# Softmax division moved into the matrix that transposes P, in two attention stages of a fused fp32 block

## The reference, cut to what matters

```
# block 1: 6 query heads, 2 key/value heads, window of +-128, blocks of 128 queries see up to 3 blocks of keys
scores = einsum(q * 64**-0.5, k) + bias
m = maximum(max(scores), sink)                  # sink: one learned logit per head
p = exp(scores - m)
p = p / (sum(p) + exp(sink - m))
out = einsum(p, v)
# block 2, mixer A: 8 heads with a sink, causal window of 128 (up to 2 blocks of keys)
# block 2, mixer B: 8 heads without a sink, causal over all 1024 keys with a table of logits (up to 8 blocks)
```

## Time and profile before

| | us |
|---|---|
| median of 3 runs (lowest, highest) | 3511.18 (3509.3, 3518.65) |
| the profiled execution: its own time | 3517.96 |
| its span | 3516.2 |
| `att_bi`, from the first scores to the last value product | about 417 to 528 in the span |
| `att_ab`, band heads | about 2258 to 2362 |
| `att_ab`, wide heads | about 2362 to 2554 |

### The profile page before, as it was taken

How to read it: one execution, slowest core, us unless ns; L and a number is a source line. 1 busy time by engine, 2 the same in 40 slices (tenths; PEclk the granted TensorE clock), 3 DMA queues, 4 the chain that set the end, 5 groups by cost and what they waited for, 6 DMA issues and landing times.

```text
span 3516.2 us, 40420 instructions
## 1 busy us (share of the span) xinstructions
PE 3244.8 (92%) x15143; PEld 2633.6 (75%) x15143; DVE 1805.5 (51%) x2429; ACT 1213.0 (34%) x2329; POOL 1656.6 (47%) x1159
## 2 busy tenths in 40 slices
PE   6978889899999999999999999888898999999987
PEld 3865568677777787788887888866677788887875
DVE  6879662878885225655522131365526655532133
ACT  3135362444442113333412130265513334312132
POOL 3321116655557667644476642210056644476652
PEclk8989899999999999999999999998899999999998
DMA  5524414322324432223245234444242223245232
GB/s 189 117 99 137 122 49 174 126 90 72 123 75 147 185 122 78 85 78 126 72 161 209 96 124 138 150 109 120 60 165 67 86 78 126 72 161 211 104 125 86
DMA packets 286911, 414.58 MB, mean 118 GB/s; under 512 B 26536, under 2 KB 211051, under 8 KB 285589
## 3 DMA queue, kind: packets, MB, share of 16 engines
q1 hardware_dynamic: 218968, 240.41, 22.8%
q10 hardware_dynamic: 62812, 154.67, 11.6%
q0 software_dynamic: 4960, 17.22, 1.5%
HBM read 324.79 MB, written 93.75 MB: 119 GB/s over the span
## 4 chain that ended last, share of the span: by engine, by line
PE 71%; DVE 15%; ACT 7%; issue 4%; DMA 2%; ACTq 1%; POOL 1%; SPq 0%; DVEq 0%; POOLq 0%
PE PS L900 63%; PE PS L2361 4%; DVE pl_ab L2478 1%; DVE cset L1340 1%; DVE ss L1216 1%; DVE cset L1338 1%; DMA w_raw<-ffn_w_down 1%; DVE pt L769 1%; PE PS L836 1%; ACT ph_ab L2412 1%; PE PS L2344 1%; DVE h_lo L894 1%; ACT pr_ab L2399 1%; ACT act L743 1%; DVE cset L1452 1%
## 5 line engine op out<-in xcount | busy, mean ns | idle before, releaser
L1244 POOL TENSOR_TENSOR sl<-ss,sh 128x512 fp32r<-128x512 f32 x300 | 436.4, 1460 | 478.6 <-ACT sh L1231 477.4
L290 POOL TENSOR_TENSOR w_lo<-w_raw,w_hi 128x512 fp32r<-128x512 f32 x460 | 641.0, 1425 | 16.0
L286 POOL CAST w_hi<-w_raw 128x2048 fp32r<-128x2048 f32 x115 | 226.9, 1973 | 658.1 <-DMA w_raw<-w_in 200.3
L1452 DVE TENSOR_TENSOR cset<-cset,PS 128x512 f32<-128x512 f32 x360 | 236.3, 684 | 403.2 <-PE PS L900 355.7
L900 PE MATMUL PS<-h_hi,sh 128*128 128x512 f32 x960 | 378.8, 395 | 27.2 <-ACT cset L1390 25.3
L900 PE MATMUL PS<-h_lo,sh 128*128 128x512 f32 x960 | 376.3, 392 | 0.0
L900 PE MATMUL PS<-h_hi,sl 128*128 128x512 f32 x960 | 376.2, 392 | 0.0
L971 DVE TENSOR_TENSOR a_lo<-aT,a_hi 128x1024 fp32r<-128x1024 f32 x66 | 104.2, 1582 | 487.6 <-ACT a_hi L968 487.6
L900 PE MATMUL PS<-w_hi,a_hi 128*128 128x512 f32 x1056 | 329.3, 393 | 19.6 <-POOL w_lo L290 14.8
L1231 ACT ACTIVATE sh<-ss 128x512 fp32r<-128x512 f32 x285 | 180.1, 632 | 478.5 <-DVE ss L1216 478.2
L900 PE MATMUL PS<-w_lo,a_hi 128*128 128x512 f32 x1056 | 328.1, 392 | 0.0
(11 more groups left out here) (362 smaller groups left out, 6348.6 us busy)
## 6 DMA issues: line engine op xcount, KB each, us to landing
w_raw<-ffn_w_down SPq DMA_DIRECT2D x88, 512.0 KB, 4.2
sr<-ffn_w_gu SPq DMA_DIRECT2D x80, 512.0 KB, 5.1
ad<-cset ACTq DMA_DIRECT2D x66, 512.0 KB, 3.1
w_raw<-w_down SPq DMA_DIRECT2D x44, 512.0 KB, 4.3
xs<-px ACTq DMA_DIRECT2D x40, 512.0 KB, 2.6
sr<-w_up SPq DMA_DIRECT2D x40, 512.0 KB, 5.1
aT<-ad ACTq DMA_DIRECT2D x3, 5632.0 KB, 17.2
w_raw<-w_out SPq DMA_DIRECT2D x32, 512.0 KB, 4.4
```

Of the source, the lines that this page charges most:

```text
L286: e.tensor_copy(w_hi[b][:, 0:n], w_raw[b][:, 0:n]).then_inc(S("w_hi"), 1)
L290: op = e.tensor_tensor(w_lo[b][:, s], w_raw[b][:, s], w_hi[b][:, s].bitcast(F32), ALU.subtract)
L1244: e.tensor_tensor(s.lo[p][:], src, s.hi[p][:].bitcast(F32), ALU.subtract).then_inc(S("s_op"), 1)
L1452: e.tensor_tensor(out, out, PS[:, b, :], op).then_inc(S("s_ev"), 1)
```

## The change

The reciprocal is taken for each unit: DVE `share(m)`, between `score(m + 1)` and `low_(m - 1)`. POOL `diagonal(m)` writes `dg[m % 2]`, the identity times the unit's 128 reciprocals. PE multiplies `pr` by this matrix instead of transposing it with `ident`: an ordinary fp32 matmul. The result is P transposed and divided. So `sinks`, `denom`, `spread`, `spread_out`, `scale`, `rr` and `t` go. The sink is a column more of `pr` that POOL `sink_column(m)` writes ahead of the exponential. The values come out of PSUM ready: ACT `y_high` and DVE `y_low` write 64 rows each for every group. For that v is loaded with both halves of its 128 columns alike. The transposed P has three banks (4, 5, 7). `out_pe` waits at its start for the last but four of these splits, and for the last one only where it needs it.

```diff
             def turn_p(m):
                 d, b, k0, k1, chunks = s.units[m]
-                e.wait_ge(S("at_exp"), n + m + 1)
+                e.wait_ge(S("at_dg"), n + m + 1)
                 for q, c0, c1 in chunks:
-                    wait(e, S("at_lo"), s.ch0 + q - 1)
+                    if q >= 3:
+                        e.wait_ge(S("at_lo"), s.ch0 + q - 2)
+                    elif q == 2 and s is att_bi:
+                        e.wait_ge(S("gl_s"), 3)
                     for k in range(c0, c1):
-                        mm = e.transpose(PS[:, 4 + q % 2, (k - c0) * P:(k - c0 + 1) * P],
-                                         a.pr[m % 3][:, (k - k0) * P:(k - k0 + 1) * P], ident[:])
+                        mm = e.matmul(PS[:, TURN_BANK[q % 3], (k - c0) * P:(k - c0 + 1) * P],
+                                      a.pr[m % 3][:, (k - k0) * P:(k - k0 + 1) * P], a.dg[m % 2][:], start=True, stop=True)
                     mm.then_inc(S("at_tr"), 1)
...
             def y_high(g):
                 d = s.units[4 * g][0]
-                e.wait_ge(S("at_nrm"), g_ + g + 1)
-                e.activation(HI(d.slot, g % 2), a.t[g // 4 % 2][:, g % 2, :], ACT.Copy)\
-                 .then_inc(S("at_yh"), 1)
+                e.wait_ge(S("at_pv"), g_ + g + 1)
+                r = slice(d.half * HD, (d.half + 1) * HD)
+                e.activation(HI(d.slot, g % 2)[r], PS[r, 6, :], ACT.Copy).then_inc(S("at_yh"), 1)
...
-                if m % 4 == 0 and g:
-                    spread_out(g - 1)
-                if m % 4 == 2 and g and (g - 1) % 4 >= 2:
+                if m % 4 == 1 and g:
                     y_high(g - 1)
...
+            def share(m):
+                e.wait_ge(S("at_exp"), n + m + 1)
+                e.reciprocal(ast[:, RD, m % 8:m % 8 + 1], ast[:, DEN, m % 8:m % 8 + 1]).then_inc(S("at_rd"), 1)
...
                 if m + 2 < s.n:
                     score(m + 2)
-                if m % 4 == 1 and m > 1:
-                    scale(m // 4 - 1)
+                if m + 1 < s.n:
+                    share(m + 1)
+                if m % 4 == 2 and m > 2:
+                    y_low(m // 4 - 1)
                 low_(m)
...
+            def diagonal(m):
+                e.wait_ge(S("at_rd"), n + m + 1)
+                if m >= 2:
+                    e.wait_ge(S("at_tr"), s.unit_end(m - 2))
+                e.tensor_scalar(a.dg[m % 2][:], ident[:], ast[:, RD, m % 8:m % 8 + 1], None, ALU.mult).then_inc(S("at_dg"), 1)
+
+            sink_column(0)
+            sink_column(1)
+            e.wait_ge(S("w_used"), (G_OUT2 if s.z else G_OUT1)[0])
+            for m in range(s.n):
+                diagonal(m)
+                if m + 2 < s.n:
+                    sink_column(m + 2)
+                if s is att_bi and 1 <= m < 7:
+                    gated_low_pool(e, m - 1)
```

More of the change, by code:

```diff
@@ L1062, in out_act @@
         def out_act(e, p):
-            e.wait_ge(S("at_yl"), 6 if p == 0 else 22)
+            e.wait_ge(S("at_yl"), 12 if p == 0 else 44)
             if p == 0:
@@ L2363, in values @@
                 mm.then_inc(S("at_pv"), 1)
-            def spread(g):
-                e.wait_ge(S("at_rd"), g_ + g + 1)
-                wait(e, S("at_rc"), g_ + g)
-                for k in range(4):
-                    r = 4 * (g % 2) + k
-                    mm = e.transpose(PS[:, 7, k * P:(k + 1) * P], ast[:, RD, r:r + 1].to_broadcast([P, P]), ident[:])
-                mm.then_inc(S("at_r"), 1)
             if s is att_ab:
@@ L2383, in att_pe @@
                     turn_p(m)
-                else:
-                    spread(m // 4 - 1)
                 if m % 4 == 3:
@@ L2392, in att_pe @@
                     tab_pe(e, m - 12)
-            spread(s.n // 4 - 1)
         def exps(e, s, a, m):
-            _, _, k0, k1, _ = s.units[m]
-            x, r, n = a.pr[m % 3][:, 0:(k1 - k0) * P], m % 8, s.h0 * TT
+            d, _, k0, k1, _ = s.units[m]
+            w, r, n = (k1 - k0) * P, m % 8, s.h0 * TT
             e.wait_ge(S("at_s"), n + m + 1)
+            if d.sink is not None:
+                e.wait_ge(S("at_sk"), n + m + 1)
+                w += 1
+            x = a.pr[m % 3][:, 0:w]
             e.activation(x, x, ACT.Exp, scale=-1.0, bias=ast[:, NM, r:r + 1], accum_out=ast[:, DEN, r:r + 1])\
@@ L2477, in low_, with y_low @@
                     o = (slice(None), slice(c0 - kb0, c1 - kb0), slice(b % 4 * P, (b % 4 + 1) * P))
[L2478 removed]
+                    e.tensor_tensor(a.pl[o], PS[:, TURN_BANK[q % 3], 0:(c1 - c0) * P].rearrange("p (k n) -> p k n", n=P),
                                     a.ph[o].bitcast(F32), ALU.subtract).then_inc(S("at_lo"), 1)
[L2481 to L2498 removed]
+            def share(m):
+                e.wait_ge(S("at_exp"), n + m + 1)
+                e.reciprocal(ast[:, RD, m % 8:m % 8 + 1], ast[:, DEN, m % 8:m % 8 + 1]).then_inc(S("at_rd"), 1)
+            def y_low(g):
+                d = s.units[4 * g][0]
+                e.wait_ge(S("at_yh"), g_ + g + 1)
+                r = slice(d.half * HD, (d.half + 1) * HD)
+                e.tensor_tensor(LO(d.slot, g % 2)[r], PS[r, 6, :], HI(d.slot, g % 2)[r].bitcast(F32), ALU.subtract)\
+                 .then_inc(S("at_yl"), 1)
             score(0)
             score(1)
+            share(0)
             if s is att_bi:
@@ L2514, in att_dve, with sink_column @@
                     tab_dve(e)
-                if m % 4 == 3:
-                    denom(m // 4)
-            scale(s.n // 4 - 1)
+            y_low(s.n // 4 - 1)
         def att_pool(e, s, a):
-            if s is att_bi:
-                for q in range(6):
-                    gated_low_pool(e, q)
-            for g in range(s.n // 4):
-                if g % 4 < 2:
-                    continue
-                d = s.units[4 * g][0]
-                e.wait_ge(S("at_yh"), s.h0 + (g // 4) * 2 + g % 2 + 1)
-                e.tensor_tensor(LO(d.slot, g % 2), a.t[g // 4 % 2][:, g % 2, :], HI(d.slot, g % 2).bitcast(F32), ALU.subtract).then_inc(S("at_yl"), 1)
+            n = s.h0 * TT
+            def sink_column(m):
+                d, _, k0, k1, _ = s.units[m]
+                if d.sink is not None:
+                    e.wait_ge(S("at_s"), n + m + 1)
+                    e.tensor_copy(a.pr[m % 3][:, (k1 - k0) * P:(k1 - k0) * P + 1], nsk[:, d.sink:d.sink + 1]).then_inc(S("at_sk"), 1)
+            def diagonal(m):
[12 more added lines that the diff above has]
+                    gated_low_pool(e, m - 1)
         nsk = at("nsk", [P, 14], F32, R3 + 6720)
```

84 lines of the change are left out of this document (28 added, 56 removed).

## The result

The changed kernel takes **3560.82 us** (median of 4 runs, 3559.62 to 3562.86), the kernel before beside it 3510.24 us: a ratio of 1.0147, 95% interval 1.0117 to 1.0177, 51 us slower. The profiled execution has a span of 3558.2 us against 3516.2, 42 us more.

The account below looks back on a forecast made before the run. The prediction took a chain of hand-overs of P between engines, none full, as the bound. Its terms 13 + 9 + 6 + 2 - 4 + 1 gave +27 us, forecast 3537 us, own range 3522 to 3552, with neighbours 3503 to 3567.

Parts of the forecast that it names:

- the neighbour with the dearer diagonal: Rival forecast: POOL's diagonal takes 0.8 us, adding 33 us, for 3570 us; chance 0.15.
- Part 1: 540 transposes of P become fp32 matmuls: net +40 us if all on the path, 0 if none.
- Part 2: Exponential to transposed P, now through reciprocal and diagonal: +6 us in the band heads, +9 in att_bi's groups 3 to 12.
- Part 3: First units of att_bi: POOL's six gated subtractions get in the diagonals' way, +13 us, the largest single term.
- the ring: Units 1 to 6 of att_bi: copy, gated_act, subtraction, diagonal, matmuls wait on each other in turn, 3.7 us a round.
- Part 4: Eight wide heads: later starts against three banks and a higher clock, +0.2 us a head, +2 us in all.
- the 2:1 weighing: Wide heads: clock up (-0.7 us a head) weighed 2:1 against clock as before (+2.2).
- Part 5: Ends and starts of the attention stretches: out_pe starts at once, -4 us; first P goes the longer way twice, +1.
- ACT sets the pace: Rival: in the groups ACT's own row of instructions is the chain, so the change is faster, 3498 us; chance 0.12.
- The clock comes up: Rival: matmuls for transposes raise the clock in the attention stretches, so no change, 3518 to 3511 us; chance 0.16.
- The diagonal is expensive: Rival: at 0.8 us on POOL the diagonal adds 33 us over rounds and groups, 3570 us; chance 0.15.

Follow-up runs that it names:

- e11: e10 with only POOL's order changed, the diagonal of unit m+2 right behind the sink column of unit m+3: 3488.08 us, ratio 0.9940 to the kernel before.
- e3: Changed kernel with matmuls by the identity instead of the diagonal, no diagonals built, division left out: 3488.34 us, ratio 0.9945 to the kernel before.
- e4: As e3, without diagonal and division, but with the old transpose in place of the fp32 matmul: 3497.39 us, ratio 0.9965 to the kernel before.
- e7: Kernel before with its transposes of P as fp32 matmuls against the identity, nothing else changed: 3504.71 us, ratio 0.9991.
- e2: Changed kernel with the diagonal built on VectorE behind the reciprocal, not on POOL: 3535.79 us, ratio 1.0084 to the kernel before.
- e10: Changed kernel with scores, exponentials, reciprocals and diagonals one unit further ahead, more buffers, gated subtractions two units later: 3522.30 us, ratio 1.0045 to the kernel before.
- e1: Changed kernel with the six gated subtractions one unit later in POOL's order: 3550.92 us, ratio 1.0123 to the kernel before.
- e8: e3 with two banks for the transposed P instead of three: 3504.28 us, ratio 0.9981 to the kernel before.
- e5: e1 with the exponential on ACT alone taken one unit earlier, ahead of the copies of unit m: 3652.30 us, ratio 1.0404 to the kernel before.
- e9: e1 with VectorE's reciprocal of unit m+1 ahead of the score step of unit m+2: 3572.51 us, ratio 1.0178 to the kernel before.

## Why the prediction was right in sign and half the size

Forecast +26 us, measured +51. 3560.8 us lies outside the forecast's own range of 3522 to 3552; it is in the wider one, 3503 to 3567, only because that takes in the neighbour with the dearer diagonal. (The sum gives +27 and 26 was added to the median, a slip of 1 us.)

**What bounds the kernel** was right: a chain of hand-overs, with no engine full. POOL's 37 us more of work in the band heads (8.7 to 45.6) cost nothing in e11 and, in the changed kernel's order, some 18.

**Part 1, the matmul for the transpose.** The price per block stands (two records). Its place was left open between 0 and +40 us; the runs put it at nothing: e3 against e4 -9, e7 against before -3 with an interval that reaches 0.

**Part 2, the way to `turn_p`** was the term that was mis-sized: +6 for the band heads came out as +17.6, +9 for `att_bi` as +13.6. Two things failed in it. The diagonal was set at 0.30 by a select of the same engine over the same tile and by a quarter of the subtraction; it took 0.60, within the bounds of 0.1 and 1.28. e2, which takes 0.32 us off and leaves POOL's queue too, puts the two together at some 15 us. The other was the counting. I wrote the late start out for one place in a group, `turn_p(8)` ahead of `values`. In the rows the wait comes at most units: TensorE's weight loads waited for POOL 87 times in the 128 units of `att_ab`, 45 of them in the 64 units of the band heads. A band group takes 7.4 us (111.0 / 15), not 6.6. And POOL's own order was not in the sum: the sink column of unit m + 2 stands before the diagonal of unit m + 1. I had put the sink columns at 0 as work "one `exps` ahead of their reader"; the work is nothing, the place in the queue was 34 us between e10 and e11. In the changed kernel itself it is 0.1 us in the group above (reciprocal ready at 2333.42, diagonal at 2333.55).

**Part 3, the ring** was found rightly, link by link, and under-sized: +13 forecast, +19.6 measured. The diagonal's missing 0.3 us makes 1.8 of the 6.6 us in six rounds. The rest is the clock, which is 0.61 from `high` of unit 1 to `high` of unit 7: three blocks take 1.61 us in the round shown where I had counted 0.67 + 0.27 at full clock, some 3.5 us in six rounds, and the first group's value products take 3.8 us (445.08 to 448.87) for the 2 us counted. I had left the fall to the range at "up to +4". e1 removes the ring by its cause, and 13.9 us of it go.

**Part 4, the wide heads.** +2 forecast, -0.7 measured, but by other amounts than I gave. The third bank is worth some 15 us (e8), the diagonal costs 14 (e3); I had them at 0.8 and 1.0 us a head, 6 and 8. The clock rose to 0.99 as the 2:1 weighing had it, but the 0.9 us a head that I had put on it did not come: with two banks the wide heads take 183.9 us at 1.00 (e8) and 184.1 at 1.00 (e7). So the small sum of this part came out by luck, from terms that were each too small or not there.

**Part 5, seams and starts.** The seams gave 6 us for 4. The start of `att_ab` cost 3.0 us; I had 1 for both starts.

**The rivals.** "ACT sets the pace" is out: ACT's busy time in the band heads fell from 62.1 to 60.1 us and the groups got longer. "The clock comes up" came true as a mechanism (0.88 to 0.99 in the wide heads) and gave no time by itself: e7, with the full clock and two records a block, takes what the kernel before takes. In the band heads and the ring the clock fell, to 0.93 and 0.61. "The diagonal is expensive" at 0.8 us, 3570, was the nearer of the neighbours: with 0.60 it would have given some 20 us over the forecast, 3557.

**Where the loss sits** is shown by undoing: the diagonal costs 72 us (e3), and as waiting, not as work, since e11 keeps the work and gets them all back; against them stand 21 us of gains, of which some 15 are the third bank's (e8) and 6 the seams'. What is left open: e11 has its gated subtractions two units later than the changed kernel, and the stretch at half clock behind the load of `relb` (16.3 us for 9.3) may be worth 7 us more, an estimate from these two rows; a run that loads `relb` earlier wasn't made.

## What to carry to other kernels

Before adding a step to a chain, write down what stands in front of it in its engine's queue, and what each of those waits for: here the same instructions cost 72 us or nothing, by the order on four engines. Take a lead on all engines of the chain at once, with the buffers that it needs; on one engine alone it becomes a wait (e5, e9, e10). And a stage whose time doesn't change may hold a gain and a loss of the same size, which only a run with one of them undone shows.
